# A hybrid convolution and latent-attention block: convolution on token-major tiles through DRAM, probabilities turned in 32x32 blocks, and another order of the first output products

## The chip, the cores and the metric

The kernel runs on 1 core of one Trainium2 chip. The metric is the device time of one execution in microseconds; lower is better. The profile is one further execution, taken by the hardware profiler on the same core. In all texts here PE is the matrix engine (TensorE), DVE is VectorE, ACT is ScalarE, POOL is GpSimd and SP is the engine that issues most DMAs.

## What is computed

One residual block on x (256 tokens by 2048), all in float32:

```python
proj = rms_norm(x) @ w_in              # u, B, C (1024 columns each), c_q 768, c_kv 512, k_rope 64
yA = B * dwconv3_causal(C * u)         # three taps per channel, then RMS norm in 8 groups of 128
yB = mla(c_q, c_kv, k_rope)            # 8 heads, chunk-causal mask, softmax, RMS norm per head
x  = x + rms_norm(concat(yA, yB) @ w_o)
x  = x + rms_norm(relu(rms_norm(x) @ w_up) ** 2 @ w_down)   # 8192 hidden columns
```

The causal convolution needs, for each token, the value of C*u one and two tokens back.

## The kernel before

**Weights.** Every weight matrix is streamed once from DRAM in "quads" of four 128-row chunks by 512 columns (1 MB) into four `raw` slots. A float32 product is made from three passes: ACT copies a half quad (two chunks) to `w_hi` (L1005), DVE writes the rest `raw - w_hi` to `w_lo` (L1305), and PE does hi*hi, hi*lo and lo*hi for two token blocks (L725 to L727). So one chunk is six matmuls of 512 columns. `w_hi` and `w_lo` hold four halves (`AHEAD = 4`): half h+4 is split as soon as PE has used half h. All instruction streams follow one list made by `plan()`. In the 96 chunk products of the six convolution strips and in the output products after them, a counter `sub` counts chunks; `between(sub)` inserts the other work ahead of chunk `sub`. The splits stand after each odd chunk. Below, "step s" is the place `sub == s`, and split(s) the split that follows chunk s. The half that split(s) makes is first read by chunk s+7.

**Attention.** Four pairs of heads; pair p starts at step 8+16p with its k/v and q products (`kv`, `q` quads), which lie between the counted chunks. Scores are made at offset 15, masked and exponentiated by DVE and ACT into `probs` (L1150, token-major). At offset 19 PE transposes `probs` into PSUM, three 128x128 blocks for each head (L748), and DVE (L1484) and ACT (L1157) copy them to `probsT`; at offset 22 PE multiplies by v (`pv`). The outputs are normalised on DVE and POOL (`o_squares`, `o_norm`), turned in 32x32 blocks by DVE into `blk`, and sent by SP through DRAM (`move_batch`: four stores to `mix_rows`, a wait, one read), and split into `yT_hi`, `yT_lo` (`o_split`).

**Convolution.** The strips come in the order u, c, b, u, c, b (512 channels each). For the first half of the channels, C*u and B are turned by DVE blocks and moved by SP (`conv_turn`, steps 38 and 54); for the second half PE transposes them (L748, steps 98 to 110). The taps then run on channel-major tiles of 128x256, eight times: ACT scales (L1190, L1186), DVE adds two taps and multiplies by B (L1520, L1524, L1526), ACT squares (L1195), PE sums over the channels of a group with a matrix of ones (L957), ACT takes the root (L1200), and DVE inverts, scales and splits (L1532 to L1536).

**Output.** The first two output strips (512 columns each) take the attention quads q=2, 3 and the convolution quads q=0, 1 in the order (strip, q) = (0,2), (0,3), (0,0), (1,2), (1,3), (1,0), (0,1), (1,1). PE waits before the first strip's quad for `oT_lo_ready` or `convT_ready`.

## Time and profile before

| | us |
|---|---|
| median of 3 runs | 1067.26 (1067.23 to 1068.05) |
| profiled execution | 1067.39 |
| its span, first to last instruction | 1065.6 |
| PE busy | 1053.6 (99%) |
| DVE busy | 695.2 (65%) |
| ACT busy | 515.9 (48%) |
| POOL busy | 80.7 (8%) |

The granted clock of TensorE is 0.997 over the span. Busy times of PE overlap from one matmul to the next, so the pace is read from the distance between starts. Idle time is given with what released it; "w_hi <- PE" is ACT waiting for a free half.

### The profile page before, as it was taken

The page shows a single profiled execution, that of the slowest core. Times are in us where ns is not written, and L with a number is a line of the kernel's source. Part 1 is how long each engine was busy: PE and PEld are TensorE (multiplying, and loading weights), DVE is VectorE, ACT ScalarE, POOL GpSimd, SP SyncE. Part 2 cuts the span into 40 slices and gives each one's busy share as a digit, 9 for nine tenths or more (in the row PEclk, how much of TensorE's full clock was granted, in tenths as well). Part 3 has the DMA queues.
Part 4 walks back from the last instruction along what each step waited for, and adds up shares of the span by engine and source line. Part 5 has one row for each costly group of instructions (what it writes and reads, how often), then busy time and mean ns, then how long its engine had stood idle before and what let it go on. Part 6 is the DMA issues. An engine that isn't in the chain of part 4 may idle for free.

```text
span 1065.6 us, 13494 instructions
## 1 busy us (share of the span) xinstructions
PE 1053.6 (99%) x4794; PEld 877.0 (82%) x4794; DVE 695.2 (65%) x785; ACT 515.9 (48%) x666; POOL 80.7 (8%) x94
## 2 busy tenths in 40 slices
PE   9999999999999999999999999999999999999996
PEld 7898888888888788888888888888888888888885
DVE  6475566679975876575575665756657656565666
ACT  7575545565544664444444444444444444444443
POOL 0011022110000310000000000000000000000003
PEclk9999999999999999999999999999999999999998
DMA  9786667864586465776666756666576665676562
GB/s 345 261 300 218 201 184 272 271 221 151 204 307 198 125 212 157 237 226 197 209 184 212 231 172 232 196 199 212 170 236 216 203 211 159 220 232 190 181 242 79
DMA packets 125619, 225.78 MB, mean 212 GB/s; under 512 B 8464, under 2 KB 30096, under 8 KB 124816
## 3 DMA queue, kind: packets, MB, share of 16 engines
q1 hardware_dynamic: 125152, 224.89, 64.7%
q10 hardware_dynamic: 432, 0.44, 0.1%
q8 instruction: 21, 0.34, 0.1%
q14 instruction: 14, 0.11, 0.0%
HBM read 210.08 MB, written 7.34 MB: 204 GB/s over the span
## 4 chain that ended last, share of the span: by engine, by line
PE 85%; issue 11%; DVE 2%; POOL 1%; DMA 1%; ACT 0%; SPq 0%; DVEq 0%; POOLq 0%; ACTq 0%
PE ps L725 28%; PE ps L727 28%; PE ps L726 28%; DMA raw<-in_w_in 1%; PE ps L748 1%; POOL acc L1666 0%; DVE w_lo L1305 0%; PE ps L909 0%; PE ps L914 0%; POOL x_res L1777 0%; POOL x_res L1751 0%; ACT w_hi L1005 0%; SPq L656 0%; DVE conv_s L1532 0%; DVEq L311 0%
## 5 line engine op out<-in xcount | busy, mean ns | idle before, releaser
L1305 DVE TENSOR_TENSOR w_lo<-raw,w_hi 128x1024 fp32r<-128x1024 f32 (+2 forms) x382 | 465.2, 1226 | 318.9 <-ACT w_hi L1005 316.8
L1005 ACT ACTIVATE w_hi<-raw 128x1024 fp32r<-128x1024 f32 (+2 forms) x382 | 395.8, 1038 | 460.7 <-PE ps L727 456.3
L725 PE MATMUL ps<-w_hi,xT_hi 128*128 128x512 f32 (+1 forms) x792 | 308.5, 390 | 0.6 <-DVE xT_lo L1406 0.5
L727 PE MATMUL ps<-w_lo,xT_hi 128*128 128x512 f32 (+1 forms) x792 | 305.9, 386 | 0.0
L726 PE MATMUL ps<-w_hi,xT_lo 128*128 128x512 f32 (+1 forms) x792 | 305.8, 386 | 0.0
L725 PE MATMUL ps<-w_hi,yT_hi 128*128 128x512 f32 x672 | 263.1, 391 | 0.0
L727 PE MATMUL ps<-w_lo,yT_hi 128*128 128x512 f32 x672 | 261.6, 389 | 0.0
L726 PE MATMUL ps<-w_hi,yT_lo 128*128 128x512 f32 x672 | 261.4, 389 | 0.0
L725 PEld LDWEIGHTS ps<-w_hi,xT_hi 128*128 128x128 f32 x792 | 148.7, 188 | 31.9 <-issue 2.0
L727 PEld LDWEIGHTS ps<-w_lo,xT_hi 128*128 128x128 f32 x792 | 148.6, 188 | 30.0
L726 PEld LDWEIGHTS ps<-w_hi,xT_lo 128*128 128x128 f32 x792 | 148.8, 188 | 28.7
L727 PEld LDWEIGHTS ps<-w_lo,yT_hi 128*128 128x128 f32 x672 | 126.1, 188 | 26.5
L726 PEld LDWEIGHTS ps<-w_hi,yT_lo 128*128 128x128 f32 x672 | 126.2, 188 | 26.1
L725 PEld LDWEIGHTS ps<-w_hi,yT_hi 128*128 128x128 f32 x672 | 126.1, 188 | 25.9
L1379 DVE TENSOR_TENSOR acc<-acc,ps 128x1024 f32<-128x1024 f32 x58 | 70.8, 1220 | 18.4 <-PE ps L727 17.5
L1685 POOL TENSOR_TENSOR a_sb<-a_sb 128x1024 f32<-128x1024 f32 x16 | 30.3, 1895 | 583.0 <-ACT a_sb L1035 583.0
L1035 ACT ACTIVATE a_sb<-ps,rstd_x 128x512 f32<-128x512 f32 x32 | 20.2, 683 | 19.9 <-PE ps L727 19.9
L1325 DVE TENSOR_TENSOR yT_lo<-aT_raw,yT_hi 128x512 fp32r<-128x512 f32 x32 | 20.6, 683 | 0.0
L1350 DVE STREAM_TRANSPOSE a_blk<-a_sb 128x512 f32<-128x512 f32 x30 | 19.5, 687 | 0.0
L1044 ACT ACTIVATE yT_hi<-aT_raw 128x512 fp32r<-128x512 f32 x32 | 18.2, 615 | 1.5 <-DVE aT_raw L1360 1.5
L1672 POOL TENSOR_TENSOR rope_c<-q_sb,cos_t 128x128 f32<-128x128 f32 x8 | 8.6, 1073 | 114.6 <-ACT q_sb L1129 114.3
L727 PE MATMUL ps<-w_lo,cqT_hi 128*128 128x384 f32 x48 | 16.1, 335 | 0.0
(155 smaller groups left out, 425.3 us busy)
## 6 DMA issues: line engine op xcount, KB each, us to landing
raw<-in_w_up SPq DMA_DIRECT2D x64, 1024.0 KB, 5.5
raw<-in_w_down SPq DMA_DIRECT2D x64, 1024.0 KB, 5.3
raw<-in_w_in SPq DMA_DIRECT2D x28, 1024.0 KB, 6.0
raw<-in_w_o SPq DMA_DIRECT2D x16, 1024.0 KB, 5.0
aT_raw<-a_blk SPq DMA_DIRECT2D x240, 32.0 KB, 1.9
raw<-in_w_uq SPq DMA_DIRECT2D x8, 576.0 KB, 4.9
mix_rows<-blk SPq DMA_DIRECT2D x32, 128.0 KB, 2.4
raw<-in_w_ukv SPq DMA_DIRECT2D x4, 1024.0 KB, 5.3
```

Source lines behind the costliest of these rows:

```text
L725: nc.tensor.matmul(dst, x_hi, hi, start=first, stop=False)
L726: nc.tensor.matmul(dst, x_lo, hi, start=False, stop=False)
L727: mm = nc.tensor.matmul(dst, x_hi, lo, start=False, stop=last)
L748: mm = nc.tensor.transpose(ps[:, bank, i * P:(i + 1) * P], src, ident[:])
L1005: nc.scalar.activation(w_hi[:, slot, 0:size], raw[:, raw_slot, first:first + size], ACT.Copy).then_inc(hi_ready, 1)
L1035: ins = nc.scalar.activation(a_sb[:, tb], ps[:, bank + tb], ACT.Relu, scale=rstd_x2[:, tb:tb + 1])
L1044: ins = nc.scalar.activation(turned(yT_hi, at, tb), blocked(tb), ACT.Copy)
L1305: nc.vector.tensor_tensor(w_lo[:, slot, 0:size], raw[:, raw_slot, first:first + size], f32(w_hi[:, slot, 0:size]), ALU.subtract).then_inc( ...
L1325: ins = nc.vector.tensor_tensor(turned(yT_lo, at, tb), blocked(tb), f32(turned(yT_hi, at, tb)), ALU.subtract)
L1350: ins = nc.vector.transpose(a_blk[:, :, tb].rearrange("p q c i -> p c q i"), a_sb[:, tb].rearrange("p (c q i) -> p c q i", c=4, q=4))
L1379: nc.vector.tensor_tensor(m, m, ps[:, bank:bank + 2], ALU.add).then_inc(acc_added, 1)
L1685: nc.gpsimd.tensor_tensor(a, a, a, ALU.mult).then_inc(a_ready, 1)
```

## The change

1. **Probabilities.** The PE transposes and both PSUM copies go. At offset 18 DVE turns `probs` in 32x32 blocks into `probsT` (128x768, `probs_turn`). At offset 20 ACT's queue stores it in four DMAs to `probs_rows` (`probs_store`), at offset 23 it reads it back into `probs` in one (`probs_read`), and at offset 26 ACT copies it in order to `probsT` (`probs_order`). `pv` moves from offset 22 to 28, and all that follows it by six: the turn of the outputs to 32, `o_split` to 42. `qrT` moves from offset 9 to 12.
2. **Convolution.** It stays token-major, in two halves of 128x1024. ACT's queue loads the taps broadcast over the partitions (`taps`, three DMAs), stores C*u to `conv_rows` behind two rows of zeros (`u_store`), and reads it back shifted by one and two rows (`u_back1`, `u_back2`). DVE does six operations of 128x1024 (`conv_mix`); ACT squares, DVE sums groups (`conv_stats`), POOL makes the reciprocal root, DVE scales (`conv_scale`) and turns (`conv_turn`, steps 93 and 105); SP moves the batch through DRAM; ACT and DVE split it (`conv_split`, steps 101 and 113). The PE transposes, the products with ones, and the roots and reciprocals of 128x256 go. ACT does one small Sqrt after the second `conv_square`.
3. **Order.** The first two strips now run (0,2), (1,2), (0,3), (1,3), (0,0), (1,0), (0,1), (1,1).
4. **Around it.** POOL clears two partitions of `blk` ahead of `ones`; SP stores them as the zero rows; SP's late loads of `g_post_mix` and `x_res` wait for `ss_c_ready` too; the rotary tiles share one tensor.

```diff
@@ plan
-        if sub in (38, 54):
-            turn("conv", sub // 54)
...
-            if at == 26:
+            if at == 32:
                 turn("o", p)
-            for when, what, h in [(9, "qrT", 0), (13, "q_order", 0), (15, "scores", 0), (15, "scores", 1),
-                                  (19, "probsT", 0), (19, "probsT", 1), (22, "pv", 0), (24, "o_squares", 0),
-                                  (25, "o_norm", 0), (36, "o_split", 0)]:
+            for when, what, h in [(12, "qrT", 0), (13, "q_order", 0), (15, "scores", 0), (15, "scores", 1),
+                                  (18, "probs_turn", 0), (20, "probs_store", 0), (23, "probs_read", 0),
+                                  (26, "probs_order", 0), (28, "pv", 0), (30, "o_squares", 0), (31, "o_norm", 0),
+                                  (42, "o_split", 0)]:
...
+        for h in range(2):
+            for when, what in [(4, "taps"), (34, "u_store"), (40, "u_back1"), (70, "u_back2")] if h == 0 else [
+                    (79, "taps"), (83, "u_store"), (88, "u_back1"), (88, "u_back2")]:
+                if sub == when:
+                    steps.append((what, h, 0))
+            for op, when in enumerate([(50, 56, 58, 76, 77, 83), (90, 91, 92, 94, 95, 99)][h]):
+                if sub == when:
+                    steps.append(("conv_mix", h, op))
+            for when, what in [[(84, "conv_square"), (86, "conv_stats"), (88, "conv_scale"), (101, "conv_split")],
+                               [(100, "conv_square"), (102, "conv_stats"), (104, "conv_scale"), (113, "conv_split")]][h]:
+                if sub == when:
+                    steps.append((what, h, 0))
+            if sub == (93, 105)[h]:
+                turn("conv", h)
...
-    order = [(0, 2), (0, 3), (0, 0), (1, 2), (1, 3), (1, 0), (0, 1), (1, 1)]
+    order = [(s, q) for q in (2, 3, 0, 1) for s in (0, 1)]
@@ scalar
+                elif what == "probs_store":
+                    act.wait_ge(probs_turned, a + 1)
                     if a:
+                        act.wait_ge(probs_landed, 16 * a)
+                    for g in range(4):
+                        act.dma_start(probs_rows[:, :, g].rearrange("q r n -> r q n"),
+                                      probs_blk[BLK * g:BLK * (g + 1)].rearrange("p q c i -> p q (c i)")
+                                      ).then_inc(probs_stored, 16)
+                elif what == "probs_read":
+                    act.wait_ge(probs_stored, 64 * (a + 1))
+                    act.dma_start(probs.rearrange("p h n -> p (h n)"), probs_rows.rearrange("q r g n -> (q r) (g n)")
+                                  ).then_inc(probs_landed, 16)
+                elif what == "probs_order":
+                    act.wait_ge(probs_landed, 16 * (a + 1))
...
+                elif what in ("u_back1", "u_back2"):
+                    back = int(what[-1])
+                    act.wait_ge(u_stored, 16 * (a + 1))
+                    act.wait_ge(zeros_stored, 16)
+                    if a:
+
+                        act.wait_ge(ss_c_ready, a)
...
+                elif what == "conv_square":
+                    act.wait_ge(conv_mixed, 6 * a + 6)
+                    nc.scalar.activation(shifted[0], u_sb[:, a], ACT.Square).then_inc(conv_sq_ready, 1)
                     if a:
...
+                        nc.scalar.activation(std_m[:], ones[:, 0:TB], ACT.Sqrt)
+                elif what == "conv_split":
+                    act.wait_ge(blk_landed, landed(("conv", a)))
...
@@ vector
+                elif what == "conv_stats":
+                    dve.wait_ge(conv_sq_ready, a + 1)
...
+                elif what == "conv_scale":
+                    dve.wait_ge(rstd_c_ready, a + 1)
...
+                elif what == "conv_split":
+                    dve.wait_ge(convT_hi_ready, a + 1)
+                    for c in range(4):
+                        k = 4 * a + c
+                        for tb in range(TB):
+                            ins = split_blocks(yT_hi[:, k], yT_lo[:, k], conv_landed(a)[:, :, tb, c], G_CONV + k, tb)
+                    ins.then_inc(convT_ready, 1)
@@ gpsimd
-            nc.gpsimd.memset(eps_col[:], EPS)
+            nc.gpsimd.memset(blk[0:2], 0.0).then_inc(zeros_ready, 1)
             nc.gpsimd.memset(ones[:], 1.0).then_inc(ones_ready, 1)
```

## Rows read from the trace of the kernel before

**Rows 1.** The page's first part: busy time, share of span, instructions.
```profile
PE 1053.6 (99%) x4794; PEld 877.0 (82%) x4794; DVE 695.2 (65%) x785; ACT 515.9 (48%) x666; POOL 80.7 (8%) x94
```

**Rows 2.** Waits of PE, whole span: total us, times, longest.
```profile
PE ps L858 <- POOL ones L1688: 1.0, 1, 1.0
PE ps L736 <- ACT w_hi L1066: 0.9, 1, 0.9
```

**Rows 3.** Timeline of PE at one pair's transposes: start, us, instruction.
```profile
122.33 0.82 PE L748 MATMUL ps<-ident,probs 128*128 128x128 f32 x6
...
123.22 0.40 PE L726 MATMUL ps<-w_hi,xT_lo 128*128 128x512 f32 x1
```

**Rows 4.** Timeline of PE at a convolution transpose group, and at a product with ones.
```profile
266.71 0.38 PE L748 MATMUL ps<-ident,u_sb 128*128 128x128 f32 x2
...
267.37 0.40 PE L726 MATMUL ps<-w_hi,yT_lo 128*128 128x512 f32 x1
...
237.60 0.60 PE L957 MATMUL ps<-conv_s,ones 128*128 128x256 f32 x2
...
238.27 0.40 PE L726 MATMUL ps<-w_hi,xT_lo 128*128 128x512 f32 x1
```

**Rows 5.** Groups by line, PE: the removed instructions and their counts.
```profile
L957 PE MATMUL ps<-conv_s,ones 128*128 128x256 f32 x16 | 4.7, 378 | 0.0
L748 PE MATMUL ps<-ident,probs 128*128 128x128 f32 x24 | 3.3, 272 | 0.0
```

**Rows 6.** Timeline of ACT at 236 to 270 us; idle before in brackets.
```profile
236.46 1.06 ACT L1005 ACTIVATE w_hi<-raw 128x1024 fp32r<-128x1024 f32 x1 [0.15 <-PE ps L727]
237.53 1.28 ACT L1200 ACT_TABLE_LOAD   x1
238.83 0.48 ACT L1200 ACTIVATE conv_s<-ps,eps_col 128x256 f32<-128x256 f32 x1
...
241.00 1.06 ACT L1005 ACTIVATE w_hi<-raw 128x1024 fp32r<-128x1024 f32 x1 [1.39 <-PE ps L727]
243.72 1.06 ACT L1005 ACTIVATE w_hi<-raw 128x1024 fp32r<-128x1024 f32 x1 [1.66 <-PE ps L727]
...
251.67 0.42 ACT L1195 ACTIVATE conv_s<-conv_y 128x256 f32<-128x256 f32 x1 [3.81 <-DVE conv_y L1526]
...
260.70 0.89 ACT L1162 ACTIVATE yT_hi<-lat,gains 128x256 fp32r<-128x256 f32 x2
...
266.90 1.06 ACT L1005 ACTIVATE w_hi<-raw 128x1024 fp32r<-128x1024 f32 x1 [0.62 <-PE ps L727]
```

**Rows 7.** Timeline of DVE at 245 to 266 us: back-to-back work and one POOL wait.
```profile
247.85 0.69 DVE L1502 TENSOR_TENSOR o_sb<-o_sb,rstd_o 128x512 f32<-128x512 f32 x1 [1.41 <-POOL rstd_o L1658]
...
264.55 1.14 DVE L1339 SCALAR_TENSOR_TENSOR yT_lo<-lat,gains,yT_hi 128x128 fp32r<-128x128 f32 x4
265.61 2.35 DVE L1305 TENSOR_TENSOR w_lo<-raw,w_hi 128x1024 fp32r<-128x1024 f32 x2
```

**Rows 8.** Busy time by stretch: span, PE, PEld, DVE, ACT, POOL, clock, DMA share, GB/s.
```profile
250.00:300.00 50.00, 50.00 (x230) 41.31 (x229) 48.55 (x69) 26.81 (x39) 0.00 (x0) 1.00 0.63 221
```

**Rows 9.** DMA issues, whole span: KB each, median us from issue to landing.
```profile
raw<-in_w_in SPq DMA_DIRECT2D x28, 1024.0 KB, 6.0
...
kqT<-mix_rows SPq DMA_DIRECT2D x6, 512.0 KB, 3.3
...
xT_raw<-in_xT SPq DMA_DIRECT2D x6, 256.0 KB, 8.8
...
g_post_mix<-in_post_mix_g SPq DMA_DIRECT2D x1, 1024.0 KB, 7.2
```

**Rows 10.** Timeline of SP's queue: one batch through DRAM, and an early load's issue.
```profile
100.31 1.77 SPq L634 DMA_DIRECT2D mix_rows<-blk  x4
104.03 0.34 SPq L647 DMA_DIRECT2D kqT<-mix_rows  x1
...
14.76 2.50 SPq L651 DMA_DIRECT2D x_in<-in_x  x1
```

More of the change, by code:

```diff
@@ L917, in step @@
                                 mm.then_inc(scores_done, 1)
-                elif what == "probsT":
-                    pe.wait_ge(probs_ready, 2 * a + b + 1)
-                    transposes((6, 7)[b], [probs[:, b, i * P:(i + 1) * P] for i in range(3)]
-                               ).then_inc(probsT_filled, 1)
                 elif what == "pv":
@@ L934, in step @@
                     mm.then_inc(pv_done, 1)
-                elif what == "convT" and a == 1:
-                    pe.wait_ge(strip_out_dve, 2)
-                    pe.wait_ge(strip_out_act, 7)
-                    pe.wait_ge(o_ready, PAIRS)
-                    if conv_bank(a, b) == conv_bank(0, 0):
-                        pe.wait_ge(conv_std_ready, 4)
-                    transposes(conv_bank(a, b), [s[:, a, tb, b * P:(b + 1) * P] for s in (u_sb, b_sb)
-                                                 for tb in range(TB)]).then_inc(convT_filled, 1)
-                elif what == "conv_norm":
-                    i = 4 * a + b
-                    pe.wait_ge(ones_ready, 1)
-                    pe.wait_ge(conv_sq_ready, i + 1)
-                    if i == 0:
-                        pe.wait_ge(probsT1_ready, PAIRS)
-                    elif a == 0:
-                        pe.wait_ge(conv_std_ready, b)
-                    nc.tensor.matmul(ps[:, conv_bank(a, b), 0:SEQ], ones[:], conv_s[:, i % NCONV, :],
-                                     start=True, stop=True).then_inc(conv_sum_done, 1)
                 elif what == "hT":
@@ new lines, in step @@
+                        act.wait_ge(conv_mixed, 4)
+                    for k in range(3):
+                        act.dma_start(conv_w[:, k], t["conv_w"][0, k:k + 1, a * W:(a + 1) * W].to_broadcast([P, W])
+                                      ).then_inc(conv_w_landed, 16)
+                elif what == "u_store":
+                    act.wait_ge(strip_out_dve, a + 1)
+                    act.dma_start(conv_rows[a, 2:2 + SEQ].rearrange("(b p) n -> p b n", p=P), u_sb[:, a]
+                                  ).then_inc(u_stored, 16)
+                elif what in ("u_back1", "u_back2"):
[4 more added lines that the diff above has]
+                        act.wait_ge(ss_c_ready, a)
+                    elif back == 1:
+                        act.wait_ge(latT_lo_ready, 3)
+                        act.wait_ge(krT_filled, 1)
+                    else:
+                        act.wait_ge(q_rope_ready, 4 * PAIRS)
+                        act.wait_ge(qrT_filled, PAIRS)
+                    act.dma_start(shifted[back - 1], conv_rows[a, 2 - back:2 - back + SEQ].rearrange(
+                        "(b p) n -> p b n", p=P)).then_inc(u_shifted[back - 1], 16)
+                elif what == "conv_square":
+                    act.wait_ge(conv_mixed, 6 * a + 6)
+                    nc.scalar.activation(shifted[0], u_sb[:, a], ACT.Square).then_inc(conv_sq_ready, 1)
+                    if a:
+                        nc.scalar.activation(std_m[:], ones[:, 0:TB], ACT.Sqrt)
[3 more added lines that the diff above has]
+                        k = 4 * a + c
+                        ins = nc.scalar.activation(by_block(yT_hi[:, k]),
+                                                   conv_landed(a)[:, :, :, c].rearrange("p g b i -> p b g i"),
+                                                   ACT.Copy, scale=gains[:, G_CONV + k:G_CONV + k + 1])
+                    ins.then_inc(convT_hi_ready, 1)
@@ L1478, in step @@
                                             ALU.mult).then_inc(neg_max_ready, 1)
[L1479 to L1480 removed]
+                elif what == "probs_turn":
+                    dve.wait_ge(probs_ready, 2 * a + 2)
                     if a:
                         dve.wait_ge(pv_done, a)
[L1484 removed]
+                    nc.vector.transpose(probs_blk.rearrange("p q c i -> p c q i"),
+                                        probs.rearrange("p h n -> p (h n)").rearrange("p (c q i) -> p c q i", c=6, q=4)
+                                        ).then_inc(probs_turned, 1)
                 elif what == "pv":
@@ L1731, in step @@
                     rstd(rstd_o, ss_o, [(slice(0, 4), V_DIM)], rstd_o_ready, 2)
+                elif what == "conv_stats":
+                    pool.wait_ge(ss_c_ready, a + 1)
+                    if a:
+                        pool.wait_ge(conv_scaled, a)
+                    rstd(rstd_c, ss_c, [(slice(0, 8), P)], rstd_c_ready, 8)
                 elif what == "y_partial":
```

173 lines of the change are left out of this document (73 added, 100 removed).

## Prediction

> **What bounds the kernel now.** I read the busy times first: PE 1053.6 us of a span of 1065.6, DVE 65%, ACT 48% [rows 1]. Then the waits of PE: the two largest are 1.0 and 0.9 us, both in the first 8 us [rows 2]. So PE is fed without a gap that counts from the first products to the last, and its own work is the time. The pace is read from the splits that PE releases: in a stretch without inserts ACT starts them at 241.00 and 243.72 [rows 6], so two chunks take 2.73 us (2.72 to the rounding), a chunk 1.365 and one 512-column matmul 0.2275. What PE no longer does comes off the end, unless a wait takes its place.
>
> **What PE loses.** In a gapless stream an insert costs the distance to the second matmul behind it, less one step. Six probability transposes: 123.22 - 122.33 - 0.23 = 0.66 us [rows 3]. There are 24 [rows 5], so 4 x 0.66 = 2.6. Four convolution transposes: 267.37 - 266.71 - 0.23 = 0.43; there are four such groups, 1.7. A product with ones, two passes: 238.27 - 237.60 - 0.23 = 0.44 [rows 4]; 16 passes are eight products [rows 5], 3.5. Sum 2.6 + 1.7 + 3.5 = **7.8 us**. Nothing is added on PE, and the new order of the output quads has the same matmuls. The profiled execution took 1067.39 us, 0.13 above the median: with no new wait it would give 1059.6, against the median 1059.5.
>
> **What could stall PE.** The cover is the lead of the splits. A half is two chunks, 2.73 us. ACT starts a split 0.2 us after the PE start that freed the slot (PE's group begins at 266.71, ACT at 266.90) [rows 4, 6] and takes 1.06; DVE then takes 1.23, or 1.13 of queue time back to back (two in 2.35) [rows 6, 7]. The half is ready 2.4 us after the release and needed three halves, 8.2 us, after it. So ACT and DVE may together lag by 5.8 us before PE waits. Both take their instructions in order, so every new wait on either is taken from these 5.8.
>
> **Probabilities, per pair.** ACT loses a 128x384 copy and gains one of 128x768, under a 128x1024 split (1.06) and over half of it; DVE loses a copy and gains a turn, about a split's length. Cover takes both. ACT's queue also issues five DMAs. Four stores cost SP 1.77 us and a read 0.34 [rows 10]; ACT gets the same. The stores go at offset 20, the read at 23. Behind the store ACT has splits; 1.8 us is within 5.8. For pairs 0 to 2 the next pair's q products lie between (six chunks of 384 columns), so the read finds the stores landed. It then has from 1.2 us behind the start of offset 22 to 1.2 behind that of 26: 5.5 us, less 0.3 to issue. The row nearest in bytes, 512 KB from DRAM by SP, lands in 3.3 us [rows 9]; this one has 384 KB. `probs_order` ends 2.1 us behind offset 26, `pv` is due 2.7 behind it: 0.6 us spare. For pair 3 no q products lie between: stores issued until 3.0 us behind the start of offset 20, landed about 2.0 later as in the batch shown (stores issued to 102.08, read issued at 104.03) [rows 10], read issued at 5.3, landed at 8.6; ACT is there at 9.4. Zero, then, with 0.6 to 0.8 us of spare each time. From both sides: nothing below zero, since PE had no wait here to lose; above, landings as in the third rival.
>
> **Convolution, first half** (steps 34 to 83). Each of its DVE operations is a 128x1024 tensor operation, 1.13 to 1.23 us like the split [rows 7], and they stand apart; the loads and shifts have tens of us. No cost. Cover gone (a shift landing late): a lag on DVE, again inside 5.8.
>
> **Where both halves meet** (steps 86 to 120). DVE was 97% busy at 250 to 300 us without a PE wait [rows 8], so sums there must be done in order. Clock t: zero at PE's start of step 86, step s at 1.365 x (s - 86). At t = 0 DVE has no lag.
> - split(85), then `o_squares` 0.65 and `conv_stats` 1.13: 4.2. `o_norm` waits for POOL, 1.41 after the sum [rows 7]; it ends at 5.1.
> - From here DVE has no gap: six splits 6.8, the output turn 0.7, `conv_scale` 1.1, the turn of half 0 (two of 0.65) 1.3, `o_split` 1.1 [rows 7], six `conv_mix` 6.9. Together 17.9: the last `conv_mix` ends at 23.0 (5.1 + 17.9). The splits on the way are in time (split(95) at 19.7, due at 21.8).
> - ACT is at the second `conv_square` at 20.3, waits for that `conv_mix` until 23.0, then squares 1.1, loads the root table 1.28, takes the small root 0.2 [rows 6], and does four copies of `conv_split(0)`, 0.45 each (two in 0.89) [rows 6]: 27.3. Behind it stands split(101).
> - DVE is idle from 24.2 to 27.3, does eight blocks of 0.27 (four in 1.06) [rows 7], then split(101): 30.7. PE wants it at 1.365 x 22 = 30.0. **Stall 0.6.**
> - `conv_stats(1)` ends at 31.8, split(103) at 32.9, POOL's root for eight columns about 2.0 (1.41 for four; I add 0.6, an estimate), `conv_scale(1)` 35.0, turn 36.3, split(105) 37.5. Due at 35.5 + 0.6 = 36.1. **Stall 1.4.**
> - The batch lands 7.0 later, as from the first store at 100.31 to the landing of the read at 107.3 (104.03 + 3.3) [rows 9, 10]: 43.3. ACT, at step 113 since 38.7, has waited; copies 1.7, DVE blocks 2.1, split(113) 48.4. Due at 46.4 + 2.0 = 48.4. Stall 0.
>
> Sum 2.0 us. Bounds: the hand sums carry about 1 us each way on a gap-free queue, so 0 to 5.5: lower if DVE saves 2 us (the stalls vanish); upper if the two shifts at step 88 cost 2.5 us each to issue, as a 1 MB load did early [rows 10], instead of 0.34, which holds ACT and starves DVE by about 1.5, and if the last batch takes 2 longer. I take the middle value because each duration has a row of its own.
>
> ACT's root table: the split before ends at 237.52, the load runs 237.53 to 238.81 and the next instruction starts at 238.83 [rows 6]. The Trainium skill ("ScalarE: Activation LUTs", section "What ACT_TABLE_LOAD costs") adds a drain of about 1.38 us to the load's 1.28. By that page the first stall would be 2.0 instead of 0.6; the trace shows the load and no drain.
>
> **The rest.** SP keeps nearly the same batches; its late loads now wait for the sum of step 102, issue behind the last batch at about t = 41 and are first needed by `y_out` after step 123 (t = 54); the gains took 7.2 [rows 9], so they are 5 us early. The second strip now starts at step 100, 5.5 us after the last B strip ends, and ACT empties that bank within 2.5. POOL's two-partition clear delays `ones`, and so the warm-up, by an estimated 0.1 to 0.9 us; PE later waits 0.9 us for the second chunk of weights [rows 2], which takes it up. Zero, bound 0.9.
>
> **Forecast.** 1067.39 - 7.8 + 2.0 = 1061.6 profiled, less 0.13 against the median: **1061.4**. About 0.2% (2.1 us) is what a measurement of this kernel can tell from no change.
>
> **Rivals.**
> - *No stall.* For it: ACT already waited 3.81 us for DVE at 251.67 [rows 6] with no PE wait; my lag beyond the cover is only 0.6 and 1.4. Against: the table load and the first half's split now stand directly behind such a wait. It gives 1059.5.
> - *DVE or ACT becomes the bound between steps 86 and 120.* For it: 48.55 of 50 us busy before [rows 8], and ACT now waits for DVE, DVE for ACT and for POOL in turn. Against: eight reciprocals and four small operations each are gone from DVE. If each of the three places is late by 2 us more, 6 more are given back: 1067, no change; two places, 1065.
> - *Reads on ACT's queue land late and hold `pv` four times: slower than before.* SP issues batches while its own weight loads are held back, and they land in 3.3; ACT's will meet 1 MB loads. Early, when many loads were in flight, 256 KB took 8.8 us [rows 9]. Pairs 0 to 2 stand 6.0 us, so 2.8 each, 8.4; pair 3, with stores landing 4 late too and its read at 9.3, is ready at 19.0 against 10.9: 8. With the forecast that gives 1078. It decides against the change from 5.8 us of such stalls, about 1.5 a pair. Against: with the DMA share at 0.63 [rows 8], a weight load itself lands in 6.0, and these transfers have under half its bytes. The Trainium skill ("DMA: Bandwidth & Descriptors", sections "Queues, rings and completion order" and "Issuing engines are not separate DMA queues") says that the queues of SP and ACT share the same 16 DMA engines, which take turns between them; no row here shows two queues at once, and by that rule a 384 KB read beside a load would about double its transfer part, some 1.5 us more, which the room of 6.0 still holds.
>
> **Chances.** Forecast (stalls 1 to 4 us) 0.45; no stall 0.30; queues as bound 0.15; late reads 0.10. Faster by over 0.2% means under 1065.1: the first two and half of the third, 0.83. Within 0.2%: the rest of the third and a little of the fourth, 0.09. Slower: 0.08. The range runs from 1058.8 (no stall, less 0.7 for inserts read too small) to 1066.0.
>
> **What would show it.** In the profile after, PE should have some 7.8 us less of transposes and products with ones. The waits of PE should list w_lo near step 108 and step 112 (about t = 30 and 36 behind step 86), 0.6 and 1.4 us, and none at `pv`. ACT should wait 2 to 3 us at the second square for the last `conv_mix`. If PE waits for `probs_order` (probsT), the DMA part is wrong; if it never waits, my DVE sum is too long; if the span falls by less than the waits explain, the inserts were mis-read.

## The result: slower by 0.9%, and the profile after

| | before | after |
|---|---|---|
| median | 1067.29 us | 1077.3 us (1075.18 to 1077.91) |
| profiled execution | 1067.39 | 1077.28 |
| its span | 1065.6 | 1075.5 |
| PE busy | 1053.6 | 1050.6 |

The ratio is 1.0087, 95% interval 1.0075 to 1.0100. The prediction was 1061.4 with a range to 1066.0. So it was wrong, in sign and by 16 us.

The page of the changed kernel, first busy time by engine, then the clock of PE in 40 slices, then ACT's own DMA queue (packets, MB, share):

```profile
PE 1050.6 (98%) x4738; PEld 872.7 (81%) x4738; DVE 686.6 (64%) x761; ACT 510.5 (47%) x649; POOL 89.9 (8%) x98
...
PEclk9999999998999999999999999999999999999998
...
q10 hardware_dynamic: 5808, 8.29, 2.3%
```

PE has the 56 fewer matmuls that were to go (4794 to 4738, [rows 1]). PE's busy time is no measure of the gain, because it contains matmuls at half the clock, as is shown below. The waits of PE over the whole span (total us, times, longest):

```profile
PE ps L939 <- ACT probsT_sb L1151: 6.0, 3, 4.5
PE ps L738 <- DVE w_lo L1314: 3.5, 2, 2.0
PE ps L922 <- DMA kqT<-mix_rows: 2.6, 2, 1.8
PE ps L871 <- POOL ones L1707: 1.9, 1, 1.9
```

Against two waits of 1.0 and 0.9 us before [rows 2], there are `pv` waiting for `probs_order` (L1151), the splits (L1314), and the scores waiting for the turned keys and queries (`kqT`, L922). Pairs count from 0. The same waits in order of time (PE's timeline: start, us, instruction, idle before it and releaser; the rows are `pv` of pair 1, the scores of pair 2, `pv` of pair 2, the scores of pair 3, `pv` of pair 3, then steps 108 and 112):

```profile
179.69 0.46 PE L939 MATMUL ps<-v_sb,probsT_sb 128*128 128x128 f32 x2 [1.10 <-ACT probsT_sb L1151]
186.39 1.55 PE L922 MATMUL ps<-kqT,lat 128*128 128x128 f32 x8 [0.79 <-DMA kqT<-mix_rows]
218.87 0.46 PE L939 MATMUL ps<-v_sb,probsT_sb 128*128 128x128 f32 x2 [0.42 <-ACT probsT_sb L1151]
226.56 1.55 PE L922 MATMUL ps<-kqT,lat 128*128 128x128 f32 x8 [1.80 <-DMA kqT<-mix_rows]
251.36 0.77 PE L939 MATMUL ps<-v_sb,probsT_sb 128*128 128x128 f32 x2 [4.49 <-ACT probsT_sb L1151]
289.91 0.50 PE L738 MATMUL ps<-w_hi,yT_hi 128*128 128x512 f32 x1 [1.49 <-DVE w_lo L1314]
297.66 0.50 PE L738 MATMUL ps<-w_hi,yT_hi 128*128 128x512 f32 x1 [1.97 <-DVE w_lo L1314]
```

A wait delays the stream by about 0.3 us more than its bracket: a matmul's modelled end lies 0.39 behind its start where the next start is 0.23 behind it, and the first start after a wait is some 0.1 slower.

**Where the time went.** The kernels issue the same weight matmuls, so the start of the same matmul can be compared in both traces:

| start of the same matmul, before | after | difference | what lies between |
|---|---|---|---|
| 50.95 | 50.97 | +0.02 | the start |
| 166.75 | 165.43 | -1.32 | two pairs' transposes gone |
| 202.88 | 203.21 | +0.33 | waits 1.10 and 0.79; pair 2's transposes gone |
| 240.80 | 241.27 | +0.47 | waits 0.42 and 1.80; pair 3's transposes and one product with ones gone, pair 3's `pv` (1.35) not yet done |
| 252.15 | 261.06 | +8.91 | pair 3: wait 4.49, half clock, its `pv`; one product with ones gone |
| 289.03 | 297.66 | +8.63 | the convolution's transposes and five products with ones gone; waits 1.49 and 1.97 |
| 381.85 | 391.69 | +9.84 | half clock behind 297.66; the last product with ones gone |

From there on the two run in step. As a sum: 7.8 off; the two waits for `kqT` and the `pv` waits of pairs 1 and 2, with their restarts, about 5.0 on; the `pv` wait of pair 3, 4.8; the two `w_lo` waits 4.0; and half clock 2.8 + 1.7 (next). That is +10.5 against +9.8 seen; 0.7 is left unexplained.

**The half clock.** PE's windows of 2 us around pair 3 (columns as in [rows 8]):

```profile
250.00:252.00 2.00, 0.64 (x3) 0.67 (x4) 2.00 (x6) 1.74 (x2) 0.00 (x0) 0.63 1.00 303
252.00:254.00 2.00, 2.00 (x12) 2.00 (x11) 2.00 (x2) 0.99 (x2) 0.00 (x0) 0.50 0.99 342
254.00:256.00 2.00, 2.00 (x7) 1.61 (x6) 0.94 (x3) 0.12 (x1) 0.87 (x1) 0.50 1.05 408
256.00:258.00 2.00, 2.00 (x7) 1.57 (x7) 0.00 (x0) 0.00 (x0) 0.17 (x1) 0.66 0.96 304
258.00:260.00 2.00, 2.00 (x11) 1.65 (x10) 0.37 (x1) 1.06 (x1) 0.00 (x0) 1.00 0.78 300
```

The granted clock falls to 0.50, the 1.2 GHz level, at about 250.5, still in the wait (251 to 252 alone is 0.50), and comes back at about 257.4. From 251.36 on PE is "busy" throughout, with x7 in 2 us (254 to 258) where full pace shows x11. The timeline shows it by the distance of starts, 0.43 at first and 0.23 at the end:

```profile
254.49 0.63 PE L739 MATMUL ps<-w_hi,xT_lo 128*128 128x512 f32 x1
254.91 0.63 PE L740 MATMUL ps<-w_lo,xT_hi 128*128 128x512 f32 x1
...
257.66 0.39 PE L738 MATMUL ps<-w_hi,xT_hi 128*128 128x512 f32 x1
257.89 0.39 PE L739 MATMUL ps<-w_hi,xT_lo 128*128 128x512 f32 x1
```

From 251.36 to 257.4 the matmuls start at a little over half pace, which costs 2.8 us. The same pitch stands from 298.56 to 301.55: seven steps with 0.20 lost on each, 1.6 to 1.7 with the two steps of the change of pace.

**Pair 3 in its queues.** ACT, with its queue of DMAs:

```profile
234.31 2.95 ACT L989 ACTIVATE w_hi<-raw 128x1024 fp32r<-128x1024 f32 x3
239.27 1.79 ACTq L1142 DMA_DIRECT2D probs_rows<-probsT_sb  x4
241.16 1.07 ACT L989 ACTIVATE w_hi<-raw 128x1024 fp32r<-128x1024 f32 x1 [3.90 <-issue]
244.01 0.34 ACTq L1147 DMA_DIRECT2D probs<-probs_rows  x1
...
246.07 2.00 ACT L989 ACTIVATE w_hi<-raw 128x1024 fp32r<-128x1024 f32 x2 [3.85 <-issue]
...
250.26 0.84 ACT L1151 ACTIVATE probsT_sb<-probs 128x768 f32<-128x768 f32 x1 [1.39 <-DMA probs<-probs_rows]
```

Step 76 starts at 235.8 on PE. ACT then still works off three splits that stood behind the softmax; DVE's turn, at 238.27, ends at 239.2. So the stores are issued up to 241.06, 2.2 us later than the 3.0 that I had. They are down at 244.0, 2.9 behind the issue (I had 2.0). The read is down at 250.24, 6.2 behind its start (I had 3.3). Together 14.4 us behind step 76 against my 8.6: 5.8 late, less some 1.4 of spare, is the 4.49 that PE waits. What lies beside it is SP's queue: one load of 1 MB at 241.08, then three more, of which the first two (241.77 and 248.4) are issued before the read has landed. The DMA share is 1.04 to 1.05 from 244 to 250 us, while the read is under way (first SP's queue, then one window, columns as above):

```profile
241.08 0.65 SPq L612 DMA_DIRECT2D raw<-in_w_in  x1
241.77 12.79 SPq L612 DMA_DIRECT2D raw<-in_w_o  x3
```

```profile
246.00:248.00 2.00, 0.87 (x4) 0.38 (x2) 0.84 (x1) 1.93 (x3) 0.00 (x0) 1.00 1.05 401
```

These loads come together because the change holds them back. SP's queue works in order, and the change moved the batch of each pair's outputs six steps later. SP issues no load between 223.5 and 241.08, since it waits for pair 2's output turn until 237.27 and then sends that batch; from 234 to 238 us the DMA share is 0.00. In the kernel before, loads stand at 227.0, 231.5, 236.1 and 244.6, and the share is 0.14 from 240 to 246 us and 0.52 from 244 to 250. No run moves this batch alone. SP's waits for turned blocks over the whole span were 25.0 us, 5.3 at the longest; here they are (total us, times, longest):

```profile
SPq L641 <- DVE blk L1345: 66.1, 11, 11.7
```

Landings over the whole span (KB each, median us) say the same for all pairs, and show that the weight loads pay too (6.0 to 7.3, [rows 9]):

```profile
raw<-in_w_in SPq DMA_DIRECT2D x28, 1024.0 KB, 7.3
...
kqT<-mix_rows SPq DMA_DIRECT2D x6, 512.0 KB, 3.7
...
probs_rows<-probsT_sb ACTq DMA_DIRECT2D x16, 96.0 KB, 5.6
probs<-probs_rows ACTq DMA_DIRECT2D x4, 384.0 KB, 6.1
```

The single reads took 4.8, 7.5, 6.0 and 6.2 us. The `kqT` waits come from the same place one queue over. SP reads a batch back when its stores are down; for pair 2 that took 1.95 us in the kernel before (issued to 177.94, read at 179.89) and takes 4.4 here, with a DMA share of 1.05 from 174 to 178 us against 0.47 before:

```profile
174.62 2.72 SPq L641 DMA_DIRECT2D mix_rows<-blk  x4
181.75 0.34 SPq L654 DMA_DIRECT2D kqT<-mix_rows  x1
```

For pair 3 it is 4.9 us against 2.0. In both pairs the scores start 0.1 us behind ACT's copy of the queries, which starts when `kqT` has landed. The rotary part (`qrT`), which the change moved three steps nearer to the scores, is not what they wait for here: DVE's copy of it ends at 182.8 and 222.0, 3.6 and 4.6 us before they start.

**The convolution's chain.** ACT where both halves meet:

```profile
282.33 1.06 ACT L1199 ACTIVATE lat<-u_sb 128x1024 f32<-128x1024 f32 x1 [3.68 <-DVE u_sb L1540]
283.41 1.28 ACT L1202 ACT_TABLE_LOAD   x1
284.70 0.20 ACT L1202 ACTIVATE std_m<-ones 128x2 f32<-128x2 f32 x1
284.81 1.69 ACT L1207 ACTIVATE yT_hi<-b_sb,gains 128x256 fp32r<-128x256 f32 x4
286.41 3.88 ACT L989 ACTIVATE w_hi<-raw 128x1024 fp32r<-128x1024 f32 x4
```

This is the predicted sequence: the wait for the last `conv_mix`, the square, the table, four copies, and four splits that had queued up. It ends in the two waits at 289.91 and 297.66.

The Trainium skill ("ScalarE: Activation LUTs", "What ACT_TABLE_LOAD costs") has a drain of about 1.38 us besides the load; here too the load starts 0.02 behind the square and the next instruction 0.01 behind the load, so no run shows a drain.

### The profile page after: what moved, and what is told of

It is laid out like the page before. It is cut to its first block, busy times and chain, and to the rows that moved or that the text cites. A ratio compares the mean times of both kernels' runs of the same rounds, so it can differ in the third digit from the quotient of the medians.

```text
span 1075.5 us, 13372 instructions
## 1 busy us (share of the span) xinstructions
PE 1050.6 (98%) x4738; PEld 872.7 (81%) x4738; DVE 686.6 (64%) x761; ACT 510.5 (47%) x649; POOL 89.9 (8%) x98
## 4 chain that ended last, share of the span: by engine, by line
PE 78%; issue 8%; DMA 5%; DVE 4%; POOL 2%; ACT 2%; SPq 1%; ACTq 0%; DVEq 0%; POOLq 0%
PE ps L738 26%; PE ps L740 26%; PE ps L739 26%; DMA raw<-in_w_in 2%; DVE w_lo L1314 1%; DMA mix_rows<-blk 1%; ACT w_hi L989 1%; DMA kqT<-mix_rows 1%; DMA probs<-probs_rows 1%; POOL acc L1685 0%; DVE u_sb L1540 0%; DVE blk L1345 0%; POOL rstd_c L1677 0%; DMA probs_rows<-probsT_sb 0%; SPq L641 0%
## 5 line engine op out<-in xcount | busy, mean ns | idle before, releaser
L1314 DVE TENSOR_TENSOR w_lo<-raw,w_hi 128x1024 fp32r<-128x1024 f32 (+2 forms) x382 | 465.5, 1227 | 333.0 <-ACT w_hi L989 331.0
L738 PE MATMUL ps<-w_hi,cqT_hi 128*128 128x384 f32 x48 | 16.1, 335 | 0.0
```

Of the source, the lines that this page charges most:

```text
L738: nc.tensor.matmul(dst, x_hi, hi, start=first, stop=False)
L1314: nc.vector.tensor_tensor(w_lo[:, slot, 0:size], raw[:, raw_slot, first:first + size], f32(w_hi[:, slot, 0:size]), ALU.subtract).then_inc( ...
```

## The experiments

My theory after the result (A): the probabilities' DMAs land late because they share the DMA engines with the weight loads; PE waits for them and for `kqT`, and loses clock behind the long wait. The convolution's two waits are a part of their own. Rivals: the stores and taps issued on ACT's queue hold ACT itself (a matter of order, not of transfers); the new order of the output products; the convolution's chain as the main cause.

| kernel | median us (range, runs) | ratio to before (95%) |
|---|---|---|
| probabilities back on PE | 1069.3 (1068.49 to 1070.68, 10) | 1.0017 (1.0007 to 1.0027) |
| probabilities alone | 1075.29 (1074.34 to 1076.16, 4) | 1.0071 (1.0054 to 1.0088) |
| taps later | 1076.36 (1075.55 to 1077.58, 4) | 1.0084 (1.0067 to 1.0101) |
| filler matmuls | 1073.35 (1072.98 to 1074.11, 4) | 1.0055 (1.0038 to 1.0072) |
| root early | 1076.28 (1074.4 to 1077.37, 4) | 1.0084 (1.0067 to 1.0101) |
| probabilities early | 1071.67 (1069.7 to 1072.14, 5) | 1.0038 (1.0024 to 1.0052) |
| root early, split late | 1073.09 (1072.8 to 1073.38, 4) | 1.0052 (1.0035 to 1.0068) |
| both of these | 1069.62 (1067.56 to 1071.54, 10) | 1.0016 (1.0007 to 1.0026) |
| half of the weights loaded | 1068.11 (1067.15 to 1070.11, 10) | 1.0006 (0.9996 to 1.0015) |
| new order alone | 1067.57 (1067.29 to 1068.29, 10) | 1.0000 (0.9991 to 1.0010) |
| all places moved | 1066.61 (1065.52 to 1067.98, 11) | 0.9991 (0.9982 to 1.0000) |
| convolution alone, tuned | 1065.72 (1064.84 to 1066.17, 11) | 0.9982 (0.9973 to 0.9991) |

Diffs are against the changed kernel unless said otherwise, and "less" is against its median of 1077.3. Beside these experiments the kernel before took 1067.6 to 1067.8, against 1067.29 in the first table, so differences of medians between the two tables carry some 0.5 us. A trace shows one execution: that of "probabilities early" took 1069.70 and that of "root early" 1074.4, each the fastest of its kernel and about 2 us under the median, so their waits may be smaller than in the other runs.

### One part alone

**Probabilities back on PE.** Part 1 undone, with its offsets (the output turn too goes back to 26, and PE's transposes and copies return); convolution, order and the rest as changed.

```diff
...
-            for when, what, h in [(12, "qrT", 0), (13, "q_order", 0), (15, "scores", 0), (15, "scores", 1),
-                                  (18, "probs_turn", 0), (20, "probs_store", 0), (23, "probs_read", 0),
-                                  (26, "probs_order", 0), (28, "pv", 0), (30, "o_squares", 0), (31, "o_norm", 0),
-                                  (42, "o_split", 0)]:
+            for when, what, h in [(9, "qrT", 0), (13, "q_order", 0), (15, "scores", 0), (15, "scores", 1),
+                                  (19, "probsT", 0), (19, "probsT", 1), (22, "pv", 0), (24, "o_squares", 0),
+                                  (25, "o_norm", 0), (36, "o_split", 0)]:
...
```

> The changed kernel with part 1 undone: probabilities transposed by PE and all offsets of a pair as before; convolution and order as changed. Theory A (the probability transfers on ACT's queue, crowding with the weight loads, are the cause): the 6.0 us of waits before pv, the 2.6 us of waits for kqT and the half-clock stretch behind the 4.5 us wait go; left are 7.8 - 2.6 = 5.2 us less PE work and the two w_lo waits near steps 108 and 112 (3.5 us) with 1.7 us of half clock behind them: about 1067, no change against the kernel before. Rival B (the convolution's own loads and shifts crowd the queue just as much): waits of several us stay in steps 30 to 84, 1071 or more.

Measured 1069.3. No wait for `pv` or `kqT` is left, and the mean granted clock is 0.997, as before the change (0.993 in the changed kernel). Four waits for `w_lo` are, 0.54, 0.52, 1.38 and 2.02 us at 269 to 291 us:

```profile
PE ps L736 <- DVE w_lo L1304: 4.5, 4, 2.0
```

So 8.0 of the 10 us go with part 1. But what is left is not the gain that 5.2 us fewer matmuls should make: 4.5 us of waits with 0.27 more for each, and 0.9 us at the start, eat it. It is 2 us above what I expected.

**Probabilities alone.** The kernel before with part 1 and the new order; PE still transposes for the convolution. Against the kernel before, what is new besides part 1 and the order:

```diff
-        if sub in (38, 54):
-            turn("conv", sub // 54)
+        if sub in (34, 50):
+            turn("conv", sub // 50)
```

> The kernel before with part 1 (probabilities by DVE and ACT's queue, later offsets) and the new order alone; convolution as before, its two turns four steps earlier so that they do not meet the output turns. PE loses 2.6 us. Theory A: waits before pv of about 1 us in pairs 1 and 2 and 2 to 4 in pair 3 stay, for pair 3 less than the 4.5 of the changed kernel because no taps are loaded beside its read: 1067 - 2.6 + 5 = 1069 to 1073. Rival B (convolution transfers are the cause): no wait before pv over 0.5 us, 1065.

Measured 1075.29, above what I expected. The `pv` waits are there, 4.62 for pair 3, although no taps are issued here, and so is the half clock (0.50 at 252 to 254), which my expectation had left out. Here alone the moved `qrT` shows: at the scores of pair 2, PE waits 0.56 us, and its copy ends last, 0.16 us behind that of the queries.

```profile
251.00 0.50 PE L930 MATMUL ps<-v_sb,probsT_sb 128*128 128x128 f32 x2 [4.62 <-ACT probsT_sb L1166]
```

**New order alone.** The kernel before, with the one line of `order` changed.

> The kernel before with the new order of the first two output strips alone. PE does the same matmuls, and no quad comes earlier than what it waits for: no wait appears, 1067.4, no change. A rival (strip 10's bank, still to be emptied by ACT at step 100, holds PE) would show a wait of 1 us or more there.

Measured 1067.57, ratio 1.0000. Part 3 costs and gains nothing that can be measured.

### What makes pair 3 late

**Taps later.** If the three tap loads, issued between the read and the splits, held ACT or the engines, moving them helps.

```diff
-                    (79, "taps"), (83, "u_store"), (88, "u_back1"), (88, "u_back2")]:
+                    (86, "taps"), (83, "u_store"), (88, "u_back1"), (88, "u_back2")]:
```

> The changed kernel with the second half's tap loads (three of 256 KB) at step 86 instead of 79, seven steps behind pair 3's read of the probabilities. If the crowding beside that read is what made it land after 6.2 us, it lands some 2 us earlier, the 4.5 us wait before pv of pair 3 falls to about 2.5 and the half clock behind it shrinks or goes: 1072 to 1075. If the weight loads alone do it, the read still takes 6 us and the time stays at 1077.

Measured 1076.36, with 4.65 us of wait at pair 3 and a read of 6.3 us. The taps are not what makes the read late.

**Half of the weights loaded.** Half of the bytes beside the reads are taken away, the instructions stay. For these quads the kernel leaves out the last two of four chunks, so PE multiplies old data there.

```diff
-                load_quad(n % RAW, quad_source(n), z["nk"], z["width"])
+                nk = 2 if 16 <= n < 60 and z["nk"] == 4 else z["nk"]
+                load_quad(n % RAW, quad_source(n)[:, 0:nk], nk, z["width"])
```

> The changed kernel with only the first two of four chunks loaded for the 1 MB weight quads 16 to 59 (the stretch of the mixer), so that half of those weights are old data; all compute instructions are the same. Theory A (weight loads in flight are what the probability transfers wait for): the reads of the probabilities land in 3.5 to 4.5 us instead of 4.8 to 7.5, the stores in about 2 to 3, the waits of pairs 1 and 2 and those for kqT go, pair 3's falls from 4.5 to about 1.5 to 2 (what is left is the late start behind the softmax), and with it the half clock: 1066 to 1069; the w_lo waits of steps 108 and 112 stay at 3.5. Rival (the queue's own order or the issue on ACT makes the landings late): 1075 or more, reads still at 6.

Measured 1068.11, 9.2 us less. Pairs 1 and 2 wait at most 0.17, `kqT` shows no wait, and the clock is 1.00 from 244 to 302 us. The landings (as above):

```profile
raw<-in_w_in SPq DMA_DIRECT2D x27, 512.0 KB, 4.5
...
probs_rows<-probsT_sb ACTq DMA_DIRECT2D x16, 96.0 KB, 3.8
probs<-probs_rows ACTq DMA_DIRECT2D x4, 384.0 KB, 4.9
```

This is the run that decides for theory A: with the same program order on ACT, fewer bytes beside it give the time back. It does not give all: reads are 4.9, not 3.3, and pair 3 waits 2.36 us. There the stores are issued 1.4 us later than in my ledger (4.4 behind step 76 for 3.0), are down 3.1 behind that and not 2.0, and the read takes 4.8. ACT, with the taps' issue (1.41 us) and four more instructions on its way, comes to `probs_order` 0.16 us before the read is down, so here the order on its queue costs nothing. The `w_lo` waits, 1.85 and 2.00, stay: they have nothing to do with the loads.

**Probabilities early.** Turn, stores and read two steps earlier; `probs_order` and `pv` stay.

```diff
-                                  (18, "probs_turn", 0), (20, "probs_store", 0), (23, "probs_read", 0),
+                                  (16, "probs_turn", 0), (18, "probs_store", 0), (21, "probs_read", 0),
```

> The changed kernel with each pair's turn, stores and read of the probabilities two steps earlier (offsets 16, 18, 21 instead of 18, 20, 23); pv stays. Theory A (each of the waits before pv is a late start on ACT and DVE plus a landing of 6 to 7.5 us beside weight loads, against a fixed room): the waits of pairs 1 and 2 (1.1 and 0.4) go, pair 3's falls by about 2 us from 4.5 to 2.5, and the half clock behind it shrinks or goes (up to 2.9 us): 1070 to 1074. The waits for kqT stay, as they come from SP's batch. Rival (the queue is full all along, so an earlier issue lands no earlier): 1077.

Measured 1071.67, 5.6 less. The reads of pairs 0 to 2 still take 5.6 to 6.8 us, so for them it is the room that was missing. Pair 3's, issued at 239.90 with a DMA share of 0.78 from 240 to 244 us, takes 3.7 for 6.2. Pair 3 waits 1.94, now because ACT itself comes late:

```profile
239.90 0.35 ACTq L1147 DMA_DIRECT2D probs<-probs_rows  x1
...
243.19 2.01 ACT L989 ACTIVATE w_hi<-raw 128x1024 fp32r<-128x1024 f32 x2 [1.78 <-DVE u_sb L1540]
245.10 0.89 ACT L1158 ACTIVATE yT_hi<-lat,gains 128x256 fp32r<-128x256 f32 x2
245.90 0.83 ACT L1151 ACTIVATE probsT_sb<-probs 128x768 f32<-128x768 f32 x1
```

The read was down at 243.6, but the taps at step 79 wait for a `conv_mix`, and the splits and `probs_order` stood behind that. With the DMAs in time, the rival about the order on ACT's queue is right after all, for these 1.94 us.

### What the half clock costs

**Filler matmuls.** 18 matmuls of 512 columns (4.1 us) into a free bank ahead of pair 3's `pv` (`FILL` is 18).

```diff
+                    if a == PAIRS - 1:
+                        pe.wait_ge(probs_ready, 2 * PAIRS)
+                        for _ in range(FILL):
+                            nc.tensor.matmul(ps[:, 7], blocks(xT_hi, 0, 0), xT_hi[:, 0:2].rearrange("p c n -> p (c n)"),
+                                             start=True, stop=True)
```

> The changed kernel with 18 extra matmuls of 512 columns (4.1 us, result not used) on PE just before it waits for pair 3's probabilities. If PE's idle time is what lets the granted clock fall to half, the wait of 4.5 becomes about 0.4, the clock stays at 1.0 in steps 84 to 86 and 2.9 us come back: 1074.4. If the clock falls for another reason, the time stays at 1077 and the half-clock stretch is still there.

Measured 1073.35, 3.95 us less with 18 matmuls more. `pv` of pair 3 waits 0.23, and the clock is 1.00 where it had been 0.50:

```profile
252.00:254.00 2.00, 2.00 (x13) 1.70 (x12) 1.97 (x4) 1.06 (x1) 0.00 (x0) 1.00 1.01 382
254.00:256.00 2.00, 2.00 (x11) 1.64 (x9) 0.60 (x1) 0.71 (x1) 1.04 (x1) 1.00 1.08 414
```

The same DVE waits follow, 1.49 and 2.00 us at 286.66 and 294.41, and this time no half clock behind them. From the `pv` of pair 3 to the first of these waits the stream gains 2.8 us on that of the changed kernel (0.48 ahead at `pv`, 3.25 at the wait). So the 2.8 is confirmed as the price of the idle time there, and the 1.7 of the later place isn't tied to the waits alone.

### The convolution's waits

**Root early.** The small Sqrt stands behind the first `conv_square`, so that the table load is not between the second one and the splits.

```diff
-                    if a:
+                    if not a:
```

> The changed kernel with the small Sqrt (and the root table load, 1.28 us) behind the first conv_square instead of the second. In the chain that ends in the first w_lo wait (last conv_mix, square, table, small root, four copies, eight blocks, split) it takes out 1.5 us, so the wait of 1.49 near step 108 should shrink to about 0.2 and the one near step 112 stay near 2 (the chain from there on starts from the same DVE work, 1.5 earlier, but PE is earlier too): about 1.5 less in all, 1075.8. Rival (the DVE backlog alone makes both waits): no change, 1077.3.

Measured 1076.28. Of the two `w_lo` waits the first is gone, and the second still has half clock behind it. From the end of pair 3's half clock to the end of the output products the delay against the kernel before goes from +7.50 to +6.97 us, where it went from +8.91 to +9.84 in the changed kernel. That is 1.5 us by the traces, the load's 1.28 and the small root; the medians, 1.0 apart with ranges that overlap, can't show it by themselves.

**Root early, split late.** As above, and `conv_split(0)` at 106 instead of 101, behind the splits that PE wants first.

> The changed kernel with the small Sqrt early and conv_split of the first half at step 106 instead of 101, so that neither stands between the last conv_mix and the splits of steps 101 to 105. By the ledger no w_lo wait over 0.3 us is left in steps 100 to 120: 3.5 us of waits, the slower restarts behind them and the second half-clock stretch of 1.7 us go: 1071.5 to 1073.5. Rival (DVE is simply overloaded there): the waits move by some steps and keep their sum, 1076 or more.

Measured 1073.09. No `w_lo` wait; but PE waits 1.71 for `conv_split(0)` itself (`yT_lo`) at 294.92: five steps were too many. Pair 3's wait (5.08) and the half clock behind it remain.

**Both.** Early probabilities with root early and split late.

> Both edits together. If the two parts are separate causes the gains add: about 1066 to 1069, near the kernel before. If they are one cause (for example one crowded queue), the sum of the gains is clearly less than that of the two alone.

Measured 1069.62: 7.7 us less, 2.1 short of the sum of 5.6 and 4.2 that the two brought singly, and 0.6 above the range expected. Left are 2.44 at pair 3 (the taps), 0.94 at `kqT`, and 2.65 at `conv_split` with 3.5 us of half clock behind it. Moved without the early probabilities, `conv_split` held PE for 1.71 us and no half clock followed; the 0.9 more and some 1.5 of half clock make up the shortfall.

### Versions

**All places moved.** Probabilities early with `probs_order` at 25, taps at 86, root early, `conv_split(0)` at 104, and POOL clears `blk` behind `ones`.

> A version: the changed kernel with turn, stores and read of the probabilities two steps earlier, probs_order at offset 25, the second half's taps at step 86, the small Sqrt behind the first conv_square, conv_split of the first half at step 104, and the clearing of blk behind ones. In the run with both edits, pair 3's pv waited 2.4 us although its read had landed: ACT stood behind the taps' wait for conv_mix; and step 112 waited 2.7 us for a conv_split placed too late. If those two are what is left, about 5.5 us more go: 1063 to 1065, faster than both kernels. If the reads stay the limit, pair 3 still waits 1 to 2 us: 1066.

Measured 1066.61, 10.7 under the changed kernel. With a ratio of 0.9991 (0.9982 to 1.0000) it is hardly told apart from the one before, and it is above the 1063 to 1065 that I expected. No `pv` waits and no half clock are left; pair 3's read lands in 3.5 us. The cost has moved to small waits, the splits in five places and `kqT`:

```profile
PE ps L738 <- DVE w_lo L1314: 2.9, 5, 0.9
PE ps L922 <- DMA kqT<-mix_rows: 1.4, 1, 1.4
```

**Convolution alone, tuned.** Against "probabilities back on PE":

```diff
-            for when, what in [[(84, "conv_square"), (86, "conv_stats"), (88, "conv_scale"), (101, "conv_split")],
+            for when, what in [[(84, "conv_square"), (86, "conv_stats"), (90, "conv_scale"), (104, "conv_split")],
...
-                    if a:
+                    if not a:
...
-            nc.gpsimd.memset(blk[0:2], 0.0).then_inc(zeros_ready, 1)
             nc.gpsimd.memset(ones[:], 1.0).then_inc(ones_ready, 1)
+            nc.gpsimd.memset(blk[0:2], 0.0).then_inc(zeros_ready, 1)
```

> Kernel: the convolution part and the new order, with the probabilities still transposed by PE as before; of the convolution part the small Sqrt stands behind the first conv_square instead of the second, conv_scale(0) at step 90 instead of 88 (so that DVE has the split of step 89 while POOL makes the root), conv_split(0) at step 104 instead of 101, and POOL clears blk behind ones instead of ahead. Theory A (the late DMA landings of the probabilities are what the change loses by; the convolution part is sound once its waits are moved): PE loses 1.7 + 3.5 = 5.2 us, no pv or kqT waits, the w_lo waits fall from 4.5 us to at most 2, and the start costs nothing: 1067.8 - 5.2 + 1 to 2, that is 1063.5 to 1064.5, the fastest of all. Rival (every place at which ACT, DVE and POOL wait for one another between steps 86 and 113 costs its lag again, wherever it is put): w_lo waits stay at 4 us and more and the time at 1067 to 1069.

Measured 1065.72, the lowest median of all and the only one whose interval lies wholly below the kernel before, but 1 to 2 us above what I expected:

```profile
269.80 0.50 PE L736 MATMUL ps<-w_hi,yT_hi 128*128 128x512 f32 x1 [1.32 <-DVE w_lo L1304]
...
273.33 0.50 PE L736 MATMUL ps<-w_hi,yT_hi 128*128 128x512 f32 x1 [0.51 <-DVE w_lo L1304]
```

The waits went from 4.5 to 2.1 us. What stays lies on DVE between steps 93 and 100 (259.5 to 269.7 us), where seven operations of 128x1024, four blocks of 128x128 and the two turns stand without a gap.

## The prediction, point by point

- **What bounds the kernel: right.** PE was the time before, and every us of difference is a wait or a clock of PE.
- **PE loses 7.8 us: right.** After two pairs' transposes the stream is 1.32 us ahead, 2 x 0.66 to the rounding. The trace of "convolution alone, tuned" bears out the other 5.2: it ends 1.97 ahead, and 5.2 less 2.1 of waits, 0.8 of restarts and 0.3 at the start is 2.0.
- **Probabilities, "zero, with 0.6 to 0.8 us of spare each time": the step that failed.** It was made of three durations taken from rows of another situation. (1) "The row nearest in bytes lands in 3.3 us": that row is SP's, whose batches run while SP itself holds back its weight loads. On ACT's queue the reads met the loads, 4.8 to 7.5 us. (2) Stores down "about 2.0 later": 2.9 for pair 3, and up to 7.4 from the issue of a single one (pair 2). (3) No lag of ACT and DVE at step 76, though the softmax's exponentials, placed at offset 15, had put three splits behind them: 2.2 us. The spare was smaller than the error of any one of them. In place of zero PE waited 6.0 us at `pv` (1.10, 0.42 and 4.49), and half clock followed the last.
- **The moved batches: not costed.** The change puts the outputs' batch six steps later in SP's queue, where it holds back the weight loads; SP waits 11.5 us for pair 2's (5.3 was its longest such wait before), and lets the loads go just ahead of pair 3's read. The prediction called SP's batches "nearly the same" and asked of them only whether they land in time.
- **The rival for this had it nearly whole.** It said 1078, from exactly this cause, at a chance of 0.10. What spoke against it was the mean DMA share of 0.63 over 50 us. Shorter windows of the kernel before show the loads about pair 1's transfers (1.04 at 168 to 174 us) and pair 2's (0.98 at 211 to 214). For pair 3 they would have said less: where its read lies, at 244 to 250 us, the share was 0.52, and it became 1.04 with the change. The rival's prices were too high for the pairs (2.8 each: measured 0, 1.1, 0.4 and, for pair 3, 4.5 instead of 8) and lacked `kqT` and the clock, so that the total of 1078 is partly luck. The Trainium skill's rule that the 16 engines take turns between the queues ("DMA: Bandwidth & Descriptors", "Queues, rings and completion order") agrees with the runs: the read went from 6.1 to 4.9 when the loads beside it were halved. The prediction's 1.5 us for it was about half of what the contention cost (a median of 6.1 against 3.3).
- **`kqT`: not costed.** The stores of SP's batches for pairs 2 and 3 took 4.4 and 4.9 us instead of 2, and the reads 3.7 instead of 3.3. Ahead of the scores there had been 1.5 and 1.4 us of spare; the waits are 0.79 and 1.80. There are none with part 1 undone and none with half the loads. The move of `qrT` from 9 to 12 is not on this path; it cost some 0.2 us in one other kernel (probabilities alone), and it wasn't run by itself.
- **The clock: not costed.** 4.5 us (2.8 and 1.7), nearly half of the 9.8.
- **Where both halves meet: right in mechanism and place, too small.** Predicted 0.6 and 1.4 at steps 108 and 112, measured 1.49 and 1.97, with 0.3 more each for the restart: 4.0 for 2.0. ACT waited 3.68 for the last `conv_mix` (predicted 2.7), and the last batch made PE wait nowhere, as forecast. Without the pairs' waits (the first experiment) there are two more of 0.5, at 269 and 273 us, at steps where I had "the splits on the way are in time". Removing the table from the path and moving the split took these away, as the ledger would have it.
- **The start: within its bound.** 0.02 us in the changed kernel, 0.87 in one experiment with the same start. It is not shown to be POOL's clear: two kernels without it show 0.20 and 0.77, two with it behind `ones` 0.06 and 0.27.
- **The order, SP's late loads: right,** no wait.

## What to carry to other kernels

A queue that does not know of the weight loads meets them: for a transfer put on a second queue, take its landing from a row with loads beside it (here about twice the undisturbed one), and look for the loads in windows of that stretch, not in a mean share. Ask too where the change itself will put them: an in-order queue that is made to wait for a later batch holds its loads back and then issues them together. For an instruction with a deadline, give it a spare larger than the uncertainty of its path, at the place with the least filling between its parts (here pair 3), and count what stands on the engine from the step before. A wait that PE did not have costs more than its length: a restart each time (0.27 us here) and, behind the waits of 4.5 to 5.1 us, the clock.

## What the runs showed of the hardware

- **Half clock behind idle time.** In all five kernels in which PE idled 4.5 to 5.1 us at pair 3 the granted clock fell to the 1.2 GHz level, in the wait or within 1 us behind it, for about 3 to 7 us; 2.8 us were lost in the changed kernel. With the gap filled it did not. Behind waits of about 2 us the traces differ: it fell behind 1.97 (changed kernel, root early), 2.11 (probabilities early) and 2.65 us (both, at `conv_split`). It did not behind 1.94 to 2.08 (taps later, fillers, on PE, half of the weights), nor behind 2.36 (half of the weights) and 2.44 (both) at pair 3. What tells them apart is open.
- **Landings beside other transfers.** A read of 384 KB took 3.5 us where the profile has it least disturbed (all places moved, pair 3), 7.5 at most in the changed kernel and 7.6 in all; 1 MB loads went from a median of 6.0 to 7.3. None of PE's waits ends with a weight load, so no direct cost of the second is seen.
- **Four stores issued by ACT** take 1.8 us of its queue at pair 3, as on SP, but 2.2, 2.1 and 3.1 at pairs 1, 2 and 0; on SP one batch took 2.7 (at 174.62), with a DMA share of 1.05.
